# A chained transformer kernel on one core: second norm without GpSimd, the first three MLP chunks side by side, and the last squared tile added by TensorE

## What is computed

```
x  = x + gate1 * (merged @ w_out)            # "wo", end of the attention part
h2 = modulate(rmsnorm(x, norm2_g), shift2, scale2)
x  = x + gate2 * (square(relu(h2 @ w_mlp_in)) @ w_mlp_out)      # MLP "m0"
x  = rmsnorm(x, final_g)
x  = x + even_mixer(rmsnorm(x)); x = x + sqrelu_mlp(rmsnorm(x)) # "even", "m1"
x  = x + odd_mixer(rmsnorm(x));  x = x + sqrelu_mlp(rmsnorm(x)) # "odd", "m2"
rmsnorm(x, g) = x * rsqrt(mean(x*x) + 1e-6) * g
```

## Time and profile before

| | |
|---|---|
| median of 3 runs | 1890.22 us (1889.25 to 1890.33) |
| profiled execution, its own time | 1891.57 us |
| span of its profile | 1889.8 us, 21055 instructions |
| PE busy | 1845.2 us (98%) |
| PEld busy | 1496.8 us (79%) |
| DVE, ACT, POOL busy | 961.5, 735.9, 44.2 us |
| DMA | 197.65 MB, mean 105 GB/s |

### The profile page before, as it was taken

One profiled execution on the slowest core, in us unless ns is written; L12 is line 12 of the kernel. 1 busy time (PEld: TensorE's weight loads), 2 busy tenths in 40 slices (PEclk: granted clock), 3 DMA queues, 4 the chain that ended last, 5 costly groups with the idle time before them and its releaser, 6 DMA issues.

```text
span 1889.8 us, 21055 instructions
## 1 busy us (share of the span) xinstructions
PE 1845.2 (98%) x8624; PEld 1496.8 (79%) x8624; DVE 961.5 (51%) x1386; ACT 735.9 (39%) x1047; POOL 44.2 (2%) x79
## 2 busy tenths in 40 slices
PE   5999999899999999999999999999999999999999
PEld 4787788678888888877888888888876788888887
DVE  7477646543434455667543434345735554344343
ACT  3365533342323243467442323243545533223231
POOL 0000000000000000011000000000001000000000
PEclk9999999899999999999999999999999999999999
DMA  8465453222222223201222222222221222222222
GB/s 283 155 187 199 156 168 121 89 85 94 100 98 101 91 95 122 79 35 45 78 90 100 98 102 90 100 90 100 89 78 34 71 97 101 95 103 93 101 89 78
DMA packets 55120, 197.65 MB, mean 105 GB/s; under 512 B 6400, under 2 KB 6656, under 8 KB 55024
## 3 DMA queue, kind: packets, MB, share of 16 engines
q1 hardware_dynamic: 52272, 188.24, 29.3%
q0 software_dynamic: 2320, 7.31, 1.4%
q10 hardware_dynamic: 432, 0.74, 0.1%
HBM read 194.13 MB, written 2.14 MB: 104 GB/s over the span
## 4 chain that ended last, share of the span: by engine, by line
PE 92%; DVE 4%; ACT 2%; issue 1%; DMA 0%; POOL 0%; SPq 0%; DVEq 0%; ACTq 0%
PE ps L298 26%; PE ps L299 26%; PE ps L300 26%; PE ps L334 2%; PE ps L335 2%; PE ps L336 2%; PE ps L419 1%; PE ps L768 1%; DVE RAW L1338 1%; PE ps L675 1%; PE ps L352 1%; PE ps L635 1%; PE ps L500 0%; DMA XT<-in_X 0%; PE ps L755 0%
## 5 line engine op out<-in xcount | busy, mean ns | idle before, releaser
L298 PE MATMUL ps<-R0h,WH 128*128 128x512 f32 x1176 | 461.7, 393 | 10.3 <-DVE R0l L1390 8.9
L865 ACT ACTIVATE WH<-RAW 128x1024 fp32r<-128x1024 f32 x299 | 313.8, 1052 | 403.5 <-PE ps L300 348.1
L1331 DVE TENSOR_TENSOR WL<-RAW,WH 128x1024 fp32r<-128x1024 f32 x299 | 365.2, 1224 | 198.3 <-ACT WH L865 194.4
L299 PE MATMUL ps<-R0l,WH 128*128 128x512 f32 x1176 | 458.5, 390 | 0.0
L300 PE MATMUL ps<-R0h,WL 128*128 128x512 f32 x1176 | 458.5, 390 | 0.0
L298 PE MATMUL ps<-R1h,WH 128*128 128x512 f32 x1064 | 417.9, 393 | 6.2 <-POOL R1l L1973 3.3
L300 PE MATMUL ps<-R1h,WL 128*128 128x512 f32 x1064 | 414.7, 390 | 0.0
L299 PE MATMUL ps<-R1l,WH 128*128 128x512 f32 x1064 | 414.7, 390 | 0.0
L298 PEld LDWEIGHTS ps<-R0h,WH 128*128 128x128 f32 x1176 | 221.3, 188 | 62.0 <-DVE R0l L1390 10.9
L300 PEld LDWEIGHTS ps<-R0h,WL 128*128 128x128 f32 x1176 | 221.2, 188 | 46.5
L299 PEld LDWEIGHTS ps<-R0l,WH 128*128 128x128 f32 x1176 | 221.4, 188 | 45.0
(11 more groups left out here) (283 smaller groups left out, 1403.4 us busy)
## 6 DMA issues: line engine op xcount, KB each, us to landing
RAW<-in_W SPq DMA_DIRECT2D x351, 512.0 KB, 3.2
XT<-in_X SPq DMA_DIRECT2D x4, 512.0 KB, 9.4
ARENA<-bias_scratch POOLq DMA_DIRECT2D x8, 256.0 KB, 4.4
XT<-in_X POOLq DMA_DIRECT2D x8, 256.0 KB, 3.5
out_x<-XT SPq DMA_DIRECT2D x8, 256.0 KB, 2.0
ARENA<-bias_scratch POOLq DMA_DIRECT2D x8, 128.0 KB, 4.1
con<-in_CON POOLq DMA_DIRECT2D x1, 578.0 KB, 7.0
CSB<-in_CV ACTq DMA_DIRECT2D x1, 512.0 KB, 5.4
```

The costliest lines, as they stand in the source:

```text
L298: e.matmul(ps(b), wh, hi, start=first, stop=False)
L299: e.matmul(ps(b), wh, lo, start=False, stop=False)
L865: e.activation(slot(n)[0], RAW[:, i % NRAW, :], ACT.Copy).then_inc(sem["w_hi"])
L1331: e.tensor_tensor(wl, RAW[:, i % NRAW, :], r32(wh), ALU.subtract).then_inc(sem["w_lo"])
```

## The change

Three things.

1. **Second norm without POOL.** Every tile takes the path that even tiles took: VectorE scales, ScalarE adds the shift and writes the high part, VectorE makes the rest. VectorE's order becomes scaled(0), scaled(1), rest(0), scaled(2), rest(1) and so on.
2. **m0's first three chunks tile by tile.** `mlp_first` runs chunks 0, 1 and 2 side by side on tiles 0 to 4 (9 matmuls a tile), then tiles 5 to 7 for chunk 0, for chunk 1 and for chunk 2. ScalarE and VectorE convert one further chunk behind each finished chunk, from the first on.
3. **The last tile's squares are not added by VectorE** in norm 1, "both", 3, 4 and 5. TensorE takes one group over SQ (six additions) and a second group over the last squared tile in TMP, in the same PSUM columns. Norm "both" so has four groups in place of two.

```diff
-            def token_sums(sq, c0, done):
+            def token_sums(sq, c0, first=False, last=False):
                 for tt in range(4):
                     t = e.matmul(PSB[6][:, c0 + tt:c0 + tt + 1], sq[:, 128 * tt:128 * tt + 128], ones1,
-                                 start=True, stop=True)
-                t.then_inc(sem[done])
+                                 start=first and tt == 0, stop=last and tt == 3)
+                return t
...
             def sums(i):
-                e.wait_ge(sem["ssq"], 7 * (i + 1))
+                e.wait_ge(sem["ssq"], 6 * i + 7)
                 open_bank(6)
-                token_sums(SQ, 0, "ss")
+                token_sums(SQ, 0, first=True)
+                e.wait_ge(sem["sq"], 8 * i + 8)
+                token_sums(TMP[:, 3, :], 0, last=True).then_inc(sem["ss"])
...
+            def mlp_first():
+                jobs = [(NO["m0i", j], WIDE[j]) for j in range(3)]
+                for ks, last in (((0,), 0), ((1,), 0), ((2,), 0), ((3,), 0), ((4,), 0), ((5, 6, 7), 1)):
+                    for j, (n, b) in enumerate(jobs):
+                        wh, wl = slot(n)
+                        for k in ks:
+                            if k == 0:
+                                e.wait_ge(sem["w_lo"], n + 1)
+                                open_bank(b)
+                            e.wait_ge(sem["h2_lo"], k + 1)
+                            w = slice(128 * k, 128 * k + 128)
+                            t = three(b, wh[:, w], wl[:, w], B[0][:, k, :], B[1][:, k, :], k == 0, k == KT - 1)
+                        if last:
+                            t.then_inc(sem["mm"])
+                            free[b] = (("mlp_rr", j + 1),)
...
             def sums_both():
-                e.wait_ge(sem["ssq"], 21)
+                e.wait_ge(sem["ssq"], 19)
                 open_bank(6)
-                token_sums(SQ, 0, "ss")
-                e.wait_ge(sem["ssqf"], 7)
-                token_sums(SQ2, 4, "ss")
+                token_sums(SQ, 0, first=True)
+                e.wait_ge(sem["ssqf"], 6)
+                token_sums(SQ2, 4)
+                e.wait_ge(sem["sq"], 24)
+                token_sums(TMP[:, 2, :], 0).then_inc(sem["ss"])
+                e.wait_ge(sem["sqf"], 8)
+                token_sums(TMP[:, 3, :], 4, last=True).then_inc(sem["ss"])
...
# ScalarE, norm2
                 for k in range(KT):
-                    j = k % 4
                     e.wait_ge(sem["nrm1"], k + 1)
-                    if k % 2 == 0:
-                        e.activation(B[0][:, k, :], TMP[:, j, :], ACT.Identity,
-                                     bias=mod_col(24 + k)).then_inc(sem["h2_hi"])
-                    else:
-                        e.activation(TMP[:, j, :], TMP[:, j, :], ACT.Identity,
-                                     bias=mod_col(24 + k)).then_inc(sem["h2_sh"])
-                        e.wait_ge(sem["h2_sh"], k // 2 + 1)
-                        e.activation(B[0][:, k, :], TMP[:, j, :], ACT.Copy).then_inc(sem["h2_hi"])
+                    e.activation(B[0][:, k, :], TMP[:, k % 4, :], ACT.Identity,
+                                 bias=mod_col(24 + k)).then_inc(sem["h2_hi"])
...
# ScalarE, mlp (VectorE's lo in the same way)
-                            if i:
-                                hi(2 if i == 1 else 1)
+                            hi()
...
# VectorE
             def ssq(i, k):
-                if k:
+                if 0 < k < 7:
                     e.wait_ge(sem["sq"], 8 * i + k + 1)
-                    e.wait_ge(sem["ssq"], 7 * i + k - 1)
+                    e.wait_ge(sem["ssq"], 6 * i + 1 + k - 1)
...
-                for k in range(0, KT, 2):
-                    scaled(k)
+                def shifted_rest(k):
                     e.wait_ge(sem["h2_hi"], k + 1)
                     e.scalar_tensor_tensor(B[1][:, k, :], TMP[:, k % 4, :], mod_col(24 + k), r32(B[0][:, k, :]),
                                            ALU.add, ALU.subtract).then_inc(sem["h2_lo"])
-                    scaled(k + 1)
+
+                scaled(0)
+                for k in range(1, KT):
+                    scaled(k)
+                    shifted_rest(k - 1)
+                shifted_rest(7)
...
# POOL
-            for k in (1, 3, 5, 7):
-                e.wait_ge(sem["h2_hi"], k + 1)
-                e.tensor_tensor(B[1][:, k, :], TMP[:, k % 4, :], r32(B[0][:, k, :]),
-                                ALU.subtract).then_inc(sem["h2_lop"])
```

More of the change, by code:

```diff
@@ L370, in norm_start @@
                 e.wait_ge(sem["ssq"], 7)
-                token_sums(xs[:, 0, :], 0, "ss")
+                token_sums(xs[:, 0, :], 0, first=True, last=True).then_inc(sem["ss"])
                 e.wait_ge(sem["rs"], RS[0] + 2)
@@ L565, in mlp @@
                         job = ((tag + "i", i), WIDE[c % 4], ("mlp_rr", MLP[tag] + i + 1))
-                        if i == 0:
+                        if norm is None:
+                            if i == 0:
+                                mlp_first()
+                            elif i > 2:
+                                gemm([job], x)
+                        elif i == 0:
                             gemm([job, ((tag + "i", 1), WIDE[1], ("mlp_rr", MLP[tag] + 2))], x, ready, mid)
-                            if norm is not None:
-                                bring(norm)
+                            bring(norm)
                         elif i > 1:
@@ L846, in tensor @@
             norm2()
-            mlp("m0", B, A, lambda k: ("h2_lop" if k % 2 else "h2_lo", k // 2 + 1), None)
+            mlp("m0", B, A, None, None)
             even()
@@ L886, in square @@
                 if k > 4:
-                    e.wait_ge(sem["ssq"], 7 * i + k - 4)
+                    e.wait_ge(sem["ssq"], 6 * i + 1 + k - 4)
                 e.activation(TMP[:, k % 4, :], XT[:, k, :], ACT.Square).then_inc(sem["sq"])
@@ L1086, in m0_then @@
                 if k > 2:
-                    e.wait_ge(sem["ssq"], 14 + k - 2)
+                    e.wait_ge(sem["ssq"], 13 + k - 2)
                 e.activation(TMP[:, j, :], XT[:, k, :], ACT.Square).then_inc(sem["sq"])
@@ L1535, in scaled @@
                 def scaled(k):
-                    if k > 4 and k % 2:
-                        e.wait_ge(sem["h2_lop"], (k - 4) // 2 + 1)
+                    if k > 3:
+                        e.wait_ge(sem["h2_lo"], k - 3)
                     e.scalar_tensor_tensor(TMP[:, k % 4, :], XT[:, k, :], gs[:, 16 + k:17 + k], ps(7), ALU.mult,
                                            ALU.mult).then_inc(sem["nrm1"])
-                for k in range(0, KT, 2):
-                    scaled(k)
+                def shifted_rest(k):
                     e.wait_ge(sem["h2_hi"], k + 1)
@@ L1559, in mlp @@
                             rest(A, n, TMP[:, j, :], ("mlp_hi", base + i + 1), "mlp_lo")
-                            if i:
-                                lo(2 if i == 1 else 1)
+                            lo()
                         else:
@@ L1591, in m0_then @@
                 fold(k, gs[:, k:k + 1], "m0")
-                if k:
+                if 0 < k < 7:
                     j, j2 = (2 * k) % 4, (2 * k + 1) % 4
                     e.wait_ge(sem["sq"], 16 + k + 1)
-                    e.wait_ge(sem["ssq"], 14 + k - 1)
+                    e.wait_ge(sem["ssq"], 13 + k - 1)
                     e.tensor_tensor(SQ[:], SQ[:], TMP[:, j, :], ALU.add).then_inc(sem["ssq"])
```

## The result

The changed kernel takes 1892.58 us, median of 21 executions (1891.10 to 1895.72); the kernel before, in executions of its own, 1889.96 (21, 1888.52 to 1891.80). The ratio is 1.0017 with a 95% interval of 1.0011 to 1.0023: slower by 2.6 us in the median and 2.9 in the mean. The forecast was 0.1 us faster, 1890.1. The result lies inside the stated range, near its upper end, which stood there for one fall of the clock.

What follows compares the result with a forecast made beforehand. The prediction took TensorE (PE), busy 98% of the span, as the bound. A gain of 4.6 us at the second norm and 4.5 us for extra groups summed to -0.1, 1890.1 us on the median; range 1887.2 to 1893.4.

Steps and rivals of the forecast that it cites:

- one fall of the clock: TensorE's clock falls once at the extra sum groups, giving 1893.4 us; chance 0.08.
- Chain: Second norm, last tile's addition removed: mean + eps from 363.79 to 363.38, a gain of 0.4 us.
- Tiles: m0's first chunks: VectorE passes of 0.75 us supply tiles faster than TensorE's demand, no wait after the first tile.
- Clock at the second norm: Second norm: TensorE's low clock level ends at the same moment as before, 372.0.
- Chunk 3: m0's chunk 3 late by 0.36 us, starting at 386.95, not 391.53; the stage gains 4.6 us.
- Groups: Norms 3, 4, 5 and both: five extra sum groups on TensorE at 0.90 us each cost 4.5 us.
- The clock falls at the extra groups: Rival, norms both and 3 to 5: one fall gives 1893.4 us (chance 0.08), two 1896.8 (two or more: 0.07).
- the extra groups are free: Rival: the extra groups' loads hide under 512-column matmuls, leaving -4.6 us alone, 1885.6; chance 0.07.
- VectorE becomes the bound: Rival, tiles behind the second norm: VectorE passes at 1.25 us add 3 us, 1893.1; chance 0.04.
- The clock never falls at the second norm: Rival: the group over SQ in idle time keeps the clock high, 2.6 us more gained, 1887.5; chance 0.12.

Runs made afterwards that it cites:

- t1: Changed kernel with VectorE adding the last tile again in norms both, 3, 4 and 5, second group in norm 1 alone: 1884.79 us, ratio 0.9978 to before.
- t2: Changed kernel with second groups in norms 1, 3, 4 and 5 only, norm both as before the change: 1888.95 us, ratio 0.9997 to before.
- t3: Changed kernel with second groups in norms 1 and both only, VectorE's addition back in norms 3, 4 and 5: 1889.53 us, ratio 1.0003 to before.
- t4: Changed kernel with the four groups of norm both set in two places, all still paid: 1891.70 us, ratio 1.0009 to before.
- c1: Kernel with the second group in norm 1 alone, plus 8 unread 512-column matmuls in place of both's extra groups: 1888.01 us, ratio 0.9988 to before.
- p1: Kernel before with only the second norm freed of POOL; chunk pair, conversions and sums as before: 1885.54 us, ratio 0.9978.
- t5: Kernel with the second group in norm 1 alone, plus 20 unread 512-column matmuls in TensorE's idle time of the second norm: 1882.81 us, ratio 0.9962 to before.
- p2: Kernel before with only m0's first three chunks tile by tile and the earlier conversions; POOL's path and sums kept: 1887.68 us, ratio 0.9986.
- after_look1: A further profiled execution of the changed kernel, nothing altered: 1891.09 us.

## Why the prediction was wrong

The steps first. *Chain:* 0.4 forecast for mean + eps, measured 0.44 (363.79 to 363.35), for the reason given. (The group over the last tile took 1.05 at the high level, not the 1.87 assumed; that changed nothing, as VectorE was the later one.) The root was at 363.53, 1.42 behind the start of the load. By that the rule that spoke against this part (the Trainium skill, "ScalarE: Activation LUTs", What ACT_TABLE_LOAD costs) fell: load and drain, 2.66 together, would have put it at 364.77. *Tiles:* no wait behind the first, VectorE's passes at 0.74 to 0.75 without POOL. *Clock at the second norm:* back at some 372.4 in the profile (0.91 over 372 to 374), 372.0 assumed. *Chunk 3:* late by 0.37, forecast 0.36. The stage gave 4.4, forecast 4.6, and 3.6 to 4.5 over the six profiled executions of the changed kernel; in these the low stretch is 10.2 us long each time and starts at different moments, from 361.9 to 364.1. *Groups:* 4.5 forecast, 4.5 measured by the rows and by the lined-up products. The sum of these steps was right to 0.2.

The step that failed is the price of the extra groups in the sum: their own time and nothing for TensorE's clock. The clock stood only in the rival "The clock falls at the extra groups", put at 0.15, with the sentence against it that the 1.7 us in a row at "both" had made no fall. Twice as long a row does: three of six profiled executions, 1.6 to 3.2 us each, 1.1 in the mean. The rival's price of a fall, 3.35, was that of a low stretch of 6.7 us. Two of the three falls lasted 3.4 us and cost 1.6, the third lasted 6.8 and cost 3.2; in both cases half of the low time.

That is not all of the miss, 2.9 in the mean where the steps give 0.1. The mean granted clock of all timed executions gives the time at the low level: 2 x (1 - clock) x span. If half of a difference in it were lost, as where PE is dense, the kernels would come out as in the fifth column. Beside it what the steps give by themselves (second norm -4.4, groups 1.8 for "both" and 0.9 for each other):

| kernel | steps | mean clock | low time, us | steps + half of extra low time | measured, mean less before |
|---|---|---|---|---|---|
| before | 0 | 0.9949 | 19.3 | | |
| changed | +0.1 | 0.9937 | 24.0 | +2.4 | +2.9 |
| t1 | -4.4 | 0.9949 | 19.2 | -4.5 | -4.5 |
| t2 | -1.7 | 0.9943 | 21.6 | -0.6 | -0.9 |
| t3 | -2.6 | 0.9938 | 23.3 | -0.6 | +0.1 |
| t4 | +0.1 | 0.9935 | 24.4 | +2.6 | +1.8 |
| c1 | -2.5 | 0.9950 | 18.9 | -2.7 | -2.2 |

(Each mean is uncertain by 0.3 to 0.4 us, the low times by 0.3 to 0.8, as the clock is given to 0.001 in each execution. Before's low time is from the executions run beside t1 to t4; beside c1 it was 19.9.) The kernels with extra one-column groups in "both" or behind it have more low time, the one with dense work in their place has not. So from kernel to kernel the loss beyond the groups' own time goes with the clock. Within one kernel it does not: six executions of the changed kernel at 1892.5 to 1892.6 have 0.995, the four at 1891.1 to 1891.5 have 0.993. One reason is in the profiles: the low stretch near 52 us counts in the mean clock and costs nothing. So the column is a sign of the clock's part in the loss, not a measurement of it.

In the profiles themselves the clock's part is shown: lined up with before's, every difference stands where an edit is or where a low stretch lies. Behind the four groups of "both" it is three of six, and one of t3's five. At the even mixer's stall all profiles with extra groups in "both" have a fall, but before's, c1's and p1's have it too, so this place is not tied to the groups.

Eight of 21 executions of the changed kernel lie at 1892.3 to 1892.6, and no profile fell among them. An estimate: a low stretch of 6.8 at the second norm and a fall of 3.4 behind "both", as t3's 1888.98 has them, would give -5.1 + 3.4 + 2.7 = +1.0 on 1891.57, or 1892.6, and with 3.4 in the even and 6.8 in the odd mixer a mean clock of 0.9946, which is written 0.995. (That execution itself gained 0.9 in the odd mixer, which the estimate leaves out.) Then all but the four executions at 1891.1 to 1891.5 had the fall. No profile shows it, so this stays open, and with it how the 1.7 us beyond the falls found are made up.

A second weakness was in the forecast's reference. Its profile was of an execution of 1891.57, 1.6 over the median of before now known, and it had a fall in the even mixer (0.86 over 800 to 812). I carried the difference of steps over to the median, as if the changed kernel would be without that fall as often. How many of before's executions have it is not shown; 1891.57 less the 1.6 that it costs is 1889.97, and the median is 1889.96. The three fastest profiled executions of the changed kernel all have that fall and are 0.3 to 0.5 under that one profile. The steps give some 0.3 over it there (-4.2 and 4.5); the rest, 0.6 to 0.7, they gain in the odd mixer, where their low stretch begins at 1383.1 to 1383.3 and before's at 1385.8. That no edit made, so their closeness to the forecast of -0.1 is in part luck.

The falls at "both" in three of six profiled executions, none in c1's, and the clock that t5 keeps at 1.0 agree with the rule that the low clock is the default and activity releases it (the Trainium skill, "TensorE: Matmul & The Clock Gate", Part 1). Of the other rivals, "the extra groups are free" fell with 0.90 a group, and "VectorE becomes the bound" with 0.75 a pass. "The clock never falls at the second norm" was put at 2.6 and gave 2.0 to 2.6, but needs dense matmuls (t5): the group over SQ alone did not keep it up in any of the six profiles of the changed kernel.

## What to carry to other kernels

Where TensorE is the bound, adding its instructions to save another engine's pays only where TensorE waits for that pass: here 0.4 us once, against 4.5 us at norms where nobody waited. Price such work at its own time and at what it may do to the clock, since a row of one-column matmuls that the page counts as busy was followed here by the low clock in some executions; where TensorE must wait, matmuls with full columns that nobody reads can be worth their slots. Two remedies for one wait don't add: try each alone first. Where executions lie in clusters, place the profiled one among the timed ones before it is taken as the base.

## What the runs showed of the hardware

- Four groups of 8 loads and 8 one-column matmuls, 3.5 us with PE 100% busy by the records, went with TensorE's low clock in four of eleven profiled executions (three of six of the changed kernel, one of five of t3), for 3.4 us three times and 6.8 once. The three short ones began 1.0 to 1.4 us behind the last group, the long one within the last two groups. Eight dense matmuls in the place of half of the groups were not followed by it, in one profile, and left the mean clock at 0.9950.
- Twenty 512-column matmuls in the second norm's idle time kept the granted clock at 1.0 in t5's profile, where it was at its low level for 10.2 us in the profile of before.
- A stall of PE of equal length (2.5 us) is followed by a fall of the clock in the profiles of some kernels and not in those of others (none in t1, t2, p2 and t5).
- A low stretch costs half of its length where PE is dense (1.6 of 3.4, 3.2 of 6.8), and 3.4 us near 52 us cost nothing that lasts, in a stretch where PE has idle time (busy 7.5 of 10 us over 50 to 60 in after_look1).
- Executions of one kernel differ by up to 4 us (1887.7 to 1891.8 for before) and lie in clusters; in the profiles of the changed kernel and of t3 the differences lie where the low stretches lie.
